# Reordering the first loads, the square-root table and the GpSimd constants at the start of a hybrid encoder layer

## The reference, cut to what matters

```
h    = rmsnorm(x, norm_mix)                 # x * rsqrt(mean(x*x) + eps) * norm_mix
proj = h @ w_in                             # 1024 x 2576, split into u_s5, qkv, z, a, b
y    = concat([s5_mixer(u_s5), gated_delta_net(qkv, z, a, b)])
x    = x + y @ w_out
x    = x + hier_moe(rmsnorm(x))             # 32 experts, top 2
out  = rmsnorm(x)
```

## Time and profile before

| | |
|---|---|
| median of 3 runs | 1410.66 us (1408.2 to 1411.42) |
| the profiled execution | 1412.43 us |
| its span in the profile | 1410.7 us |
| PE busy | 1319.2 us, 94% |
| DVE busy | 1079.2 us, 76% |
| ACT busy | 868.1 us, 62% |
| POOL busy | 462.5 us, 33% |
| mean granted TensorE clock | 0.976 of full |

### The profile page before, as it was taken

The page is one execution under the profiler, slowest core; times in us unless marked ns, Lnnn a source line. Parts: engine busy times, 40 slices in busy tenths (PEclk is TensorE's granted clock), DMA queues, the critical chain, the costliest instruction groups (busy, mean ns, idle before and its releaser), DMA issues. The chain is left out here.

```text
span 1410.7 us, 25141 instructions
## 1 busy us (share of the span) xinstructions
PE 1319.2 (94%) x8506; PEld 1113.9 (79%) x8506; DVE 1079.2 (76%) x1468; ACT 868.1 (62%) x1168; POOL 462.5 (33%) x508
## 2 busy tenths in 40 slices
PE   4999999987898889999998999999999999999995
PEld 3999778867888878758887788888888888888872
DVE  5795798684878748744666988888888888888856
ACT  7474345565566455463213877777777788777754
POOL 6020089108665637511200143333111111111125
PEclk9999999997999999999998999999999999999998
DMA  9175887512224119832103999999999999999956
GB/s 273 43 227 157 259 245 228 150 32 47 59 60 161 33 47 338 324 91 91 45 31 145 421 421 422 412 409 416 410 408 409 411 413 411 405 414 415 391 210 255
DMA packets 154825, 357.51 MB, mean 253 GB/s; under 512 B 43999, under 2 KB 100603, under 8 KB 127483
## 3 DMA queue, kind: packets, MB, share of 16 engines
q1 hardware_dynamic: 131899, 297.04, 55.9%
q0 software_dynamic: 14976, 40.43, 8.4%
q10 hardware_dynamic: 7872, 19.01, 3.4%
HBM read 287.64 MB, written 68.78 MB: 253 GB/s over the span
## 5 line engine op out<-in xcount | busy, mean ns | idle before, releaser
L2972 PE MATMUL gate_up_mm<-w_hi,gathered_T_hi 128*128 128x512 f32 x528 | 210.7, 399 | 1.1 <-DVE gathered_T_lo L3186 0.9
L2974 PE MATMUL gate_up_mm<-w_hi,gathered_T_lo 128*128 128x512 f32 x528 | 206.6, 391 | 0.0
L2973 PE MATMUL gate_up_mm<-w_lo,gathered_T_hi 128*128 128x512 f32 x528 | 206.4, 391 | 0.0
L3181 DVE TENSOR_TENSOR w_lo<-w_down,w_hi 128x2048 fp32r<-128x2048 f32 x66 | 148.5, 2290 | 54.0 <-ACT w_hi L3095 53.9
L3095 ACT ACTIVATE w_hi<-w_up 128x2048 fp32r<-128x2048 f32 x66 | 126.6, 1920 | 52.7 <-PE down_mm L3009 50.3
L3181 DVE TENSOR_TENSOR w_lo<-first_w_gate,w_hi 128x2048 fp32r<-128x2048 f32 x66 | 150.4, 2289 | 8.2 <-ACT w_hi L3095 8.2
L3181 DVE TENSOR_TENSOR w_lo<-w_up,w_hi 128x2048 fp32r<-128x2048 f32 x66 | 150.6, 2288 | 4.4 <-ACT w_hi L3095 0.6
L3095 ACT ACTIVATE w_hi<-first_w_gate 128x2048 fp32r<-128x2048 f32 x66 | 127.0, 1926 | 41.4 <-PE gate_up_mm L2974 27.4
L2847 POOL COPY gather_idx<-upto_pair 128x1 int32 x33 | 11.0, 335 | 425.6 <-PE x_turned L2962 425.6
L3095 ACT ACTIVATE w_hi<-w_down 128x2048 fp32r<-128x2048 f32 x66 | 123.9, 1916 | 38.7 <-issue 22.0
L2972 PEld LDWEIGHTS gate_up_mm<-w_hi,gathered_T_hi 128*128 128x128 f32 x528 | 99.6, 189 | 27.6 <-issue 8.3
(11 more groups left out here) (535 smaller groups left out, 3151.1 us busy)
## 6 DMA issues: line engine op xcount, KB each, us to landing
w_up<-in_expert_w_up SPq DMA_DIRECT2D x66, 1024.0 KB, 8.6
w_down<-in_expert_w_down SPq DMA_DIRECT2D x66, 1024.0 KB, 7.4
first_w_gate<-in_expert_w_gate SPq DMA_DIRECT2D x64, 1024.0 KB, 8.0
expert_rows_dram<-ones SPq DMA_DIRECT2D x32, 512.0 KB, 6.6
expert_rows_dram<-expert_out ACTq DMA_DIRECT2D x32, 512.0 KB, 8.3
x<-s_rows_dram SPq DMA_DIRECT2D x9, 1184.0 KB, 7.7
s_rows<-s_rows_dram SPq DMA_DIRECT2D x7, 1184.0 KB, 7.0
w_raw<-in_w_in SPq DMA_DIRECT2D x12, 512.0 KB, 5.3
```

What stands on the lines that cost most here:

```text
L2972: pe.matmul(dst, xT_hi[:, k, :], hi[:, at, cols], start=k == 0, stop=False)
L2973: pe.matmul(dst, xT_hi[:, k, :], lo[:, at, cols], start=False, stop=False)
L2974: mm = pe.matmul(dst, xT_lo[:, k, :], hi[:, at, cols], start=False, stop=k == KT - 1)
L3181: dve.tensor_tensor(lo[:, at, :], flat(j), hi[:, at, :].bitcast(F32), ALU.subtract).then_inc(S["piece_lo"], 1)
```

## The change

Four things are moved. The norm weight is loaded from ScalarE's queue as its first instruction. A square root of one column of `ones` is taken on ScalarE before the first square, so that the table with the root is the first that is loaded; it waits for `made` to be 1, the memset of `ones`. x comes in five loads: tile 0, tile 1, and then three of two tiles. On GpSimd only `ones` and `ident` are made before the S5 loads, the other constants after them.

```
-def make_constants(pool, c, made):
-    step = Steps(pool, made)
+def make_identity(pool, c, step):
     step(pool.memset(c["ones"][:], 1.0))
     step.done()
     one = c["ones"][:]
     step(pool.affine_select(out=c["ident"][:], in_=one, compare_op=ALU.is_equal, ...))
+def make_constants(pool, c, step):
+    one = c["ones"][:]
     ...
+X_LOADS = ((0, 1), (1, 2), (2, 4), (4, 6), (6, 8))
...
+    first_root = core.sb("x_first_root", [P, 1])
...
-            for i in range(4):
-                sp.dma_start(xs[:, 2 * i:2 * i + 2], x_rows[:, 2 * i:2 * i + 2]).then_inc(x_ld[i], 16)
-            with nc.allow_non_contiguous_dma(reason="small parameters"):
-                sp.dma_start(normw[:], a["norm_mix"][0].rearrange("(k p) -> p k", p=P)).then_inc(S["par_ld"], 16)
+            for i, (first, end) in enumerate(X_LOADS):
+                sp.dma_start(xs[:, first:end], x_rows[:, first:end]).then_inc(x_ld[i], 16)
...
-            make_constants(pool, c, made)
+            constant_step = Steps(pool, made)
+            make_identity(pool, c, constant_step)
             with nc.allow_non_contiguous_dma(reason="small parameters"):
                 s5.loads(pool)
                 t5.loads(pool)
+            make_constants(pool, c, constant_step)
...
+            with nc.allow_non_contiguous_dma(reason="small parameters"):
+                act.dma_start(normw[:], a["norm_mix"][0].rearrange("(k p) -> p k", p=P)).then_inc(S["par_ld"], 16)
+            act.wait_ge(made, 1)
+            act.activation(first_root[:], c["ones"][:, 0:1], ACT.Sqrt)
             for t in range(TT):
-                act.wait_ge(x_ld[t // 2], 16)
+                act.wait_ge(x_ld[loaded_with[t]], 16)
```

More of the change, by code:

```diff
@@ L185, in in_projection @@
     made = S["made"]
-    x_ld = [core.sem(f"pj_x_ld{i}") for i in range(4)]
+    x_ld = [core.sem(f"pj_x_ld{i}") for i in range(len(X_LOADS))]
     z_ld = [core.sem(f"pj_z_ld{i}") for i in range(KT)]
@@ L191, in in_projection @@
     x_rows = a["x"].rearrange("b (t p) d -> p (b t) d", p=P)
+    loaded_with = {t: i for i, (first, end) in enumerate(X_LOADS) for t in range(first, end)}
     w_in = a["w_in"][0].rearrange("(k p) n -> p k n", p=P)
```

## The result

The changed kernel takes 1420.7 us (median of 13 runs, 1417.96 to 1425.98) against 1411.43 us for the kernel before in the same measurement. The ratio is 1.0067, with an interval of 1.0051 to 1.0083: slower by 9.4 us, between 7.2 and 11.7. The forecast was 1417.3 us within 1410.0 to 1419.4. The direction held, and so did the main mechanism, S5 packets that delay x; the size was 1.4 times what I gave, and the time lies 1.3 us above the range. Of these 1.3 us, 0.8 are the kernel before itself, which took 1411.43 us here and 1410.66 when I forecast.

What follows compares the result with a forecast made beforehand. The bound was when TensorE's dense work begins, set by x's load. x's last pair at 13.55 + 0.5 (norm weight) + 4.6 (B) + 2.6 (C) = 21.3 us, squares 6.6 us later: 1410.66 + 6.6 = 1417.3 us, range 1410.0 to 1419.4.

Steps and rivals of the forecast that it cites:

- The chain: Before TensorE's dense work: x lands, eight squares on ScalarE, 3.35 us more, then `lo_rows` on VectorE.
- Passed on one for one: A shift of the end of the first 40 us reaches the total time in full, as later stages wait for data.
- Root first, at most 1.1 us gained: Early root takes the 1.28 us table load out of ScalarE's squares; the seventh could start at 13.55 instead of 14.69.
- The norm weight, +0.5: On ScalarE's queue its packets compete with x's load and take at most 0.5 us from it; issue taken as 0.
- B, +4.6: S5 B loads, flowing from about 8.5 us, take turns with x's packets and delay x by 4.6 us.
- C, +2.6: S5 C loads share with x's remaining packets at 0.83 packet for one, costing x 2.6 of 4.4 us.
- The upper bound, +8.4: All S5 traffic ahead of x's last packet: x lands at 23.05 us, 8.4 us later.
- The rule of the Trainium skill: DMA engines go round robin among queues, a packet at a time; by strict turns the sum would be +7.2 us.
- x isn't disturbed: Rival, 0.20: x's packets, queued first, go ahead of the S5 packets; 1409.6 to 1410.4 us, no measurable change.
- only the B loads: Rival, 0.14: only B packets get in among x's, C packets too late or too few; +4.0 us, 1414.7 us.
- faster: Rival, 0.08: gains of table load, norm weight and first tile add on the path, 4.5 us; 1406.2 us.
- More of it: Rival, 0.05: S5 packets start so early that all are ahead of x's second pair too; +8.4 us, 1419.1 us.

Runs made afterwards that it cites:

- The first four runs: Follow-ups expected together: S5 loads back behind the constants; S5 loads' move alone; norm weight back on SP; only C loads late. Ratios 1.0049, 1.0066, 1.0052, 1.0062.
- s5_on_sp: Kernel before with early root and split first tiles only, its S5 loads issued by SP behind x, norm weight and eight w_in pieces; ratio 1.0001.
- norm_on_sp: Changed kernel with the norm weight back on SP's queue behind x, S5 loads still early; ratio 1.0052.
- after_x: Changed kernel with S5 loads behind the constants and kept back until x is there, norm weight still on ScalarE's queue; only time 1413.09 us.
- half_rows: Changed kernel with x loaded in runs of 2 KB instead of 4 KB, two loads for each; only time 1421.14 us.
- s5_late: Changed kernel with the S5 loads back behind all constants, the other three moves kept; ratio 1.0049.
- root_and_tiles: Changed kernel with S5 loads back behind the constants and norm weight back on SP behind x; early root and split tiles stay; ratio 0.9989.
- best: Kernel before with early root and split first tiles, GpSimd waiting for x's last load before issuing the S5 loads; ratio 1.0004.
- s5_early_only: Kernel before with only the S5 loads moved ahead of the other constants; ratio 1.0066.

## Why the prediction was wrong

Taken by its steps:

- *The chain* (x lands, squares, 3.35 us, `lo_rows`): right. In the changed kernel the last square is out at 25.81 and `lo_rows` starts 3.34 us later. The norm weight's wait, the first tiles' early start: off the chain, as said.
- *Passed on one for one*: holds as far as these times tell. Shifts of `lo_rows` of +8.7, +7.1, +7.0, +6.8, +4.75, +2.2, +0.9, −0.8 and −1.2 us stand beside ratios of 1.0067, 1.0062, 1.0052, 1.0066, 1.0049, 1.0026, 1.0004, 0.9989 and 1.0001, and each shift lies inside the interval of its ratio. The first four runs, which share one measurement of the kernel before, all have a ratio above their shift, by 0.03 to 0.18%, so the times support "one for one" only that roughly.
- *Root first, at most 1.1 us gained*: 0.8 without the rest (1.2 in s5_on_sp, where no GpSimd issue holds the first mean); eaten by the wait for x in the changed kernel.
- *S5 loads 4.77 us earlier*: they began at 1.51 us, 4.62 earlier, with 28 packets of q0 between 8 and 9 us.
- *The norm weight, +0.5*: **mis-sized**. By 9 us x had moved 1.99 MB against 2.59 before, 0.60 MB or 1.46 us behind, of which the first small S5 packets are at most a fifth; norm_on_sp and after_x give 1.75 and 1.5. This is the step that failed: I priced its 1024 packets by what they filled when no other queue had much to send. Between 4 and 5 us, among x's, they left the engines at 74%. Strict turns don't price them either, with 724 packets to x's 35; why 4 KB of them cost 1.5 us is open. Their issue on ScalarE took 0.49 us, in the wait for x, and cost nothing, as I had taken it.
- *B, +4.6*: from 9 to 15 us x moved 0.72 MB, 1.76 us' worth, so 4.2. Right within a tenth.
- *C, +2.6*: **mis-sized**. The turns are strict here (407 to 408), which I had as a possibility and averaged away with 0.83 of a packet; that alone is 0.6 us. And x was 1 us further behind when they came. From 15 to 23 us q1 moved 1.67 MB, 4.1 us' worth of 8: 3.9 us of cost, near the whole 4.4. (The last 0.2 MB of it are w_in's, which follows x in the queue; x itself had 1.45 MB left at 15 us.)
- The sum of what was measured, 13.55 + 1.46 + 4.2 + 3.9 = 23.1, meets the 23.41 us of the seventh square; mine was 21.3. These terms are x's lost time in stretches that follow one another, so they had to add up. The check from outside is after_x, where the seventh square is 8.4 us earlier without S5 packets near x, against 4.2 + 3.9 = 8.1.
- *The upper bound, +8.4*: it took the norm weight at "at most 0.5", so the true 1.5 was outside it, and the measured +8.7 with it. The term that I gave no range of its own broke the bound; the C term, which I held open up to 4.4, was inside.
- *The rule of the Trainium skill* (DMA: Bandwidth & Descriptors, Queues, rings and completion order), round robin a packet at a time: beside the C loads the changed kernel (407 to 408) and half_rows (388 to 376) agree, if a packet is what the trace counts as one. Beside the norm weight (35 to 724) the trace does not agree with it in that sense. For the C term I should have gone by it.
- *The rivals*: "x isn't disturbed" is out (the waits of 3.54 and 2.45 us), "only the B loads" too, "faster" too. "More of it" is nearest in size, but not by its mechanism: B packets were not early.

What I had not seen at all is that the kernel before stands at an edge: x's last packets had gone just after 13.0 us, and the B packets came at 13.25. The norm weight's 1.5 us, which I added to the sum, cost the seventh square 4.1 and `lo_rows` 4.75 without the S5 loads' move (s5_late); with that move, norm_on_sp prices it at 1.75. The two moves are not additive.

No version beat the kernel before by more than the measurement can tell. root_and_tiles and s5_on_sp start `lo_rows` 0.8 and 1.2 us earlier.

## What to carry to other kernels

An early load is not free if a queue beside it feeds the critical path. Beside the C loads each queue got a packet in turn, whatever x's packets held, so what a load takes from another goes by its packets and not only by its bytes. Put what nobody waits for behind the critical load in the same queue, as s5_on_sp does. Where it stays in a queue of its own, read from the trace how many microseconds part the two, since that margin decides. Price a term at the place it will have, not at the place where the old trace happened to show it.

## What the runs showed of the hardware

**Tiny packets cost more beside others.** The norm weight's 1024 packets of 4 bytes went through in some 0.55 us behind x, all engines full (an estimate from the 930 in 0.5 us of the earlier trace rows), and cost x 1.5 us when they went among its packets (after_x; 1.75 by norm_on_sp).

**Scattered runs.** 0.5 MB in runs of 16 floats cost a queue beside it 4.2 us in the changed kernel and 4.6 in the one before; as plain rows at 0.41 MB/us it would be 1.3, an estimate.

**GpSimd's DMA issue holds VectorE.** A mean of 128 by 4 that takes 0.17 us took 0.48 (before), 0.65 (root_and_tiles), 1.28 (best) and 1.07 us (after_x), and ended each time within 0.02 us of the end of GpSimd's issue of a B load (11.32, 11.32, 17.24 and 18.49 us). Where SP issued them it took 0.17. Not every issue holds it: beside the issues of C loads the mean took between 0.17 (norm_on_sp) and 0.31 us (s5_late, s5_early_only), and why the B loads do more is not shown. The Trainium skill (SBUF — State Buffer, Terms) says that VectorE and GpSimd share a pair of ports, that the loser is blocked and not slowed; the four held means agree, and they show VectorE as the loser while GpSimd issues. That it is this port was not tested by itself.
